# An eighth place in the ring of expert weights, in the memory of the residual

## What is computed

```
pg = softmax(h @ w_rg + b_rg)                 # 4 groups, the best one is taken
sel = the 8 expert logits of that group
pe_top, e_idx = top_k(softmax(sel), 2)        # 2 of 8 experts
weights = pg_top * pe_top / sum(pe_top)
for each token and each of its 2 experts:     # 32 experts in all
    a = xb @ w_gate[ex];  u = xb @ w_up[ex]   # 1024 x 512 each
    y = (silu(a) * u) @ w_down[ex]            # 512 x 1024
    out[token] += y * weight
x = x + out
```

## Time and profile before

| | before |
|---|---|
| median of 3 runs | 3719.6 us (3717.64 to 3726.79) |
| the profiled execution | 3721.73 us |
| its span in the trace | 3719.5 us |
| part on experts, first gate stage to last down stage | 3100.8 to 3692.3 us |
| PE busy, share of the span | 89% |
| DMA, mean of the core's 16 engines over six repetitions (3201.6 to 3647.4 us) | share 0.93, 388 GB/s |

### The profile page before, as it was taken

The page is one execution under the profiler, slowest core; times in us unless marked ns, Lnnn a source line. Parts: engine busy times, 40 slices in busy tenths (PEclk is TensorE's granted clock), DMA queues, the critical chain, the costliest instruction groups (busy, mean ns, idle before and its releaser), DMA issues.

```text
span 3719.5 us, 38781 instructions
## 1 busy us (share of the span) xinstructions
PE 3326.3 (89%) x16196; PEld 2288.9 (62%) x16196; DVE 1128.7 (30%) x1781; ACT 1053.8 (28%) x1795; POOL 709.1 (19%) x344
## 2 busy tenths in 40 slices
PE   7998899987858999989889999988899988989996
PEld 5676678865537777756568876465686664333332
DVE  5333320223395555353231112375230121000001
ACT  3532342325432222123342331133321122111110
POOL 3022244432210000013134440000242221000001
PEclk9999999997879988789999999998999999999998
DMA  3231153321100000122122323210122238989996
GB/s 117 80 124 46 46 185 109 125 85 51 57 12 1 1 2 1 51 94 77 36 86 94 91 91 96 78 35 1 38 90 71 74 149 324 401 355 392 386 387 279
DMA packets 217628, 448.04 MB, mean 120 GB/s; under 512 B 14176, under 2 KB 191360, under 8 KB 204528
## 3 DMA queue, kind: packets, MB, share of 16 engines
q1 hardware_dynamic: 197664, 389.04, 28.7%
q10 hardware_dynamic: 9744, 36.18, 2.4%
q0 software_dynamic: 10048, 20.35, 1.6%
HBM read 502.14 MB, written 31.46 MB: 143 GB/s over the span
## 4 chain that ended last, share of the span: by engine, by line
PE 77%; DVE 8%; DMA 8%; ACT 3%; issue 3%; POOL 1%; SPq 0%; ACTq 0%; POOLq 0%; DVEq 0%
PE product_banks L563 13%; PE product_banks L564 12%; PE product_banks L565 12%; PE product_banks L535 8%; PE product_banks L1923 5%; DMA A<-in_w_down 4%; PE product_banks L1960 4%; DMA A<-in_w_up 3%; PE product_banks L627 3%; PE product_banks L1125 1%; PE score_banks L1106 1%; PE product_banks L1342 1%; PE product_banks L2396 1%; PE product_banks L586 1%; PE product_banks L587 1%
## 5 line engine op out<-in xcount | busy, mean ns | idle before, releaser
L472 POOL TENSOR_TENSOR Wr_parts<-Wr,Wr_parts 128x1024 fp32r<-128x1024 f32 x186 | 447.1, 2405 | 1431.9 <-ACT Wr_parts L449 1431.9
L564 PE MATMUL product_banks<-A_parts,Wr_parts 128*128 128x512 f32 x1408 | 560.0, 398 | 0.0
L449 ACT ACTIVATE Wr_parts<-Wr 128x1024 fp32r<-128x1024 f32 x186 | 196.0, 1058 | 729.8 <-PE product_banks L565 634.8
L1923 PE MATMUL product_banks<-A,Wr 128*64 128x512 f32 x1504 | 344.3, 600 | 12.9 <-DMA A<-in_w_up 11.8
L563 PE MATMUL product_banks<-H_parts,Wr_parts 128*128 128x512 f32 x728 | 298.6, 410 | 24.4 <-POOL Wr_parts L472 20.8
L564 PEld LDWEIGHTS product_banks<-A_parts,Wr_parts 128*128 128x128 f32 x1408 | 270.0, 192 | 61.7 <-issue 2.2
L563 PE MATMUL product_banks<-A_parts,Wr_parts 128*128 128x512 f32 x680 | 269.5, 396 | 31.8 <-DVE A_parts L485 15.6
L565 PE MATMUL product_banks<-H_parts,Wr_parts 128*128 128x512 f32 x728 | 292.3, 402 | 0.0
L472 POOL TENSOR_TENSOR shared_con_parts<-Wr,shared_con_parts 128x1024 fp32r<-128x1024 f32 x80 | 193.0, 2413 | 449.8 <-ACT shared_con_parts L449 449.8
L565 PE MATMUL product_banks<-A_parts,Wr_parts 128*128 128x512 f32 x680 | 267.2, 393 | 0.0
L1923 PEld LDWEIGHTS product_banks<-A,Wr 128*64 128x64 f32 x1504 | 117.2, 138 | 216.9 <-issue 213.5
(11 more groups left out here) (444 smaller groups left out, 5246.1 us busy)
## 6 DMA issues: line engine op xcount, KB each, us to landing
A<-in_w_gate SPq DMA_DIRECT2D x32, 2048.0 KB, 14.0
A<-in_w_up SPq DMA_DIRECT2D x32, 2048.0 KB, 17.8
A<-in_w_down SPq DMA_DIRECT2D x32, 2048.0 KB, 13.6
Wr<-in_m_w_up SPq DMA_DIRECT2D x32, 1024.0 KB, 5.4
Wr<-in_m_w_down SPq DMA_DIRECT2D x32, 1024.0 KB, 4.7
Wr<-in_w_in SPq DMA_DIRECT2D x32, 1024.0 KB, 5.4
Wr<-in_c_w_kv SPq DMA_DIRECT2D x16, 1024.0 KB, 5.0
expert_rows<-LB ACTq DMA_DIRECT2D x12, 1024.0 KB, 4.4
```

Source lines behind the costliest of these rows:

```text
L449: nc.scalar.activation(weight_parts(s)[0], loaded_part(s), ACT.Copy).then_inc(*mark("weights_high", s))
L472: nc.gpsimd.tensor_tensor(lo, loaded_part(s), hi, ALU.subtract).then_inc(*mark("weights_split", s))
L564: pe.matmul(bank[:, :], hi[:, k, :], x_lo, start=False, stop=False)
L1923: mm = pe.matmul(BK[r, 0 if kind == "gate" else 1, :], XT[b % 2][:, k * P + CAP * h:k * P + CAP * h + CAP], unit_rows((kind, b, h))[:, k, ...
```

## The change

The ring has eight places. The first seven units go into the same places of `A` as before, the eighth into `X`, and so on round the ring; the load of unit g now waits for the stage that used unit g-8. The eighth unit, the first to use `X`, waits for the last turn of the residual.

```
-RINGW = 7
+RINGW = 8
...
         def unit_slot(key):
-            n = 8 * ((LOAD_AT[key] + 2) % RINGW)
-            return A[:, n:n + 8, :]
+            place = (2, 3, 4, 5, 6, 0, 1, 7)[LOAD_AT[key] % RINGW]
+            return X[:, :, :] if place == 7 else A[:, 8 * place:8 * place + 8, :]
...
                      ("low_part_ready", ("merged", 7)), ("products_done", ("wout2", 7)),
-                     ("products_done", ("wout2", 7))]
+                     ("products_done", ("wout2", 7)), ("turned", ("xr", TT - 1, 1))]
```

## The result

The changed kernel takes 3692.94 us (median of 4 runs, 3689.66 to 3695.72), the kernel before 3723.19 us over 4 runs. The ratio is 0.9918, 95% interval 0.9897 to 0.9939: 0.8% or 30 us faster. 3686 was forecast, with a range of 3667 to 3705.

The account below looks back on a forecast made before the run. Neither TensorE (66.9 us) nor DMA (66.3 us) alone but their waiting for each other was taken to bound each 74.3 us repetition. 35 us over six plus 1 at the start, leaned to 34, from 3719.6 gave 3686 us, range 3667 to 3705.

Parts of the forecast that it names:

- The circle: In the six repetitions, a down unit's late load idles the DMA and delays the next down stage; 7.4 us lost each.
- rivals C and E: C: DMA's sustained rate of 388 GB/s binds, gain 8 us at most, chance 0.06. E: TensorE alone binds, 3668 us, chance 0.07.
- The size: Six repetitions of nine expert stages: period 68.5 us instead of 74.3, 35 us gained in all.
- The DMA's idle: Experts, before the gate units issued at a down stage's end: 2.1 us idle instead of 7.4 per repetition.
- Rival B: Experts: the stall moves, DMA goes dry twice a repetition, period 71.5 us, gain 17 us, 3703 us; chance 0.13.
- The circle of 10 units: From one down stage's end to the down start three blocks on: 10 units, rows and restart, 60.0 us.
- The slow stage: Down stage partly at low clock, 8.4 us: disappears if the wait before it stays under 1.4 us.
- Rival D: Experts: several short waits, each followed by a low-clock stage; period 79.8 us, 33 us slower, 3753 us; chance 0.04.
- The start: Experts before 3201.6 us, one wait of 5.21 us and a slow stage: gain 0 to 7.9 us, taken as 1.
- Cost of nothing: Reading X as a place, POOL's wait for the turns and later row loads: each 0 us; 13 us bound for X.
- The signs: Profile after: period near 68.5 us, shorter down waits, adjacent SP issues, DMA 410 to 420 GB/s; wrong if full stretches fall below 427.

## Why the prediction was right

**The place of the loss.** The circle (a down unit that waits for the down stage, which waits for its own late unit) was read from the earlier trace rows. With the second half's wait put back the gain is gone, ratio 1.000; with X as a place but seven of them it is gone too. Shown. One slip in the working: the DMA's own loss was 74.3 - 66.3 = 8.0 us a repetition; the 7.4 that the prediction gives for it is TensorE's.

**The bounds of a repetition.** 66.3 us were worked out for the DMA alone and 66.9 for TensorE alone. Measured with the other out of the way: 66.6 and 67.0. So the 7.4 us that belonged to neither were real, and rivals C and E are judged by the same two numbers: there was something to gain, and a place does not get all of it.

**The size.** 68.5 us a repetition was forecast and 69.2 measured: 30.5 us over six instead of 35; at the end I had taken 2 off. The DMA's idle was forecast at 2.1 us. It measured 69.2 - 66.6 = 2.6 us a repetition by the periods and 2.3 by the rates. The size is near, but the place is wrong in the main. I had it in front of the gate that waits for the end of down; there it is 4.0 us in six repetitions. 9.4 us lie where I had none, in front of the down units that come behind an extra block's gate and up: empty units hold four of the eight places there, and the queue is nearly empty when those two units go out. The prediction let the last unit of down 5 land 3.9 us after that moment (3258.7 against 3254.8); it landed 1.9 us after it (3255.3 against 3253.4), and the two units behind it came too late to keep the rate up. Rival B said that the DMA runs dry in two places, which is so, but its second place was in front of gate 9, and there the rate hardly falls (399 GB/s from 3286 to 3292).

The circle of 10 units lacks the same term. It gave 60.0 to 60.8 us from the end of a down stage to the start of the one three blocks on. Where TensorE did not wait that took 60.1 us, its own eight stages (3264.3 to 3324.4); where it waited it took 61.6 to 63.2 (3401.7 to 3463.2, 3331.4 to 3394.6). So four waits of 1.4 to 3.1 us remained, where the forecast had 0 to 0.8, and a slow stage in two repetitions, where it had one in all or in none. Per repetition that is 67.0 + 1.5 of waits + 0.6 of slow stages = 69.1. That 69.2 is also the value worked out for a slow stage in every repetition is luck: the terms differ and their sum agrees.

**The slow stage.** I had tied its end to a wait under 1.4 us. It ended in four of six repetitions: in two there was no wait, and in one the wait was 1.44 us. The fourth is against the rule, and against my leaning on every wait above 2 us for a slow stage: waits of 2.17 and 2.34 us were followed by stages of 8.78 us, one of 3.08 us by a stage of 7.09, with the granted clock at 1.00 in it (3394.6 to 3401.7):

```profile
3394.57 7.09 PE L1960 MATMUL product_banks<-A,Wr 128*64 128x512 f32 x32 [3.08 <-DMA A<-in_w_down]
```

Rival D, many short waits with a slow stage behind each, did not come: there are fewer waits, not more. The experiment with six places shows that its mechanism exists (waits before gate with slow stages behind), though there it is the ring that causes them.

**The start.** The stage behind the long wait of the earlier trace rows now waits 2.95 us instead of 5.21 and takes 8.78 us instead of 9.78, but the down stage of block 2 waits 2 us where it hardly did before. From the first gate stage to 3201.6, 1.6 us were gained (3102.4 to 3201.6 against 3100.8 to 3201.6), where 1 us was forecast. In this profile that gain does not reach the time, since the first gate stage itself starts 1.6 us later than in the profile before.

**Cost of nothing.** X as a place, POOL's wait for the turns, the row transfers: all 0. Loads of rows land in 10.5 us at the median, 10.8 before.

**The signs.** Period, SP's issues, share, rate and the length of stages came as listed. One did not: the wait of down was to be under 1 us in at least half of the repetitions, and it was in two of six. And by the letter one sign of being wrong did come: the rate in full stretches was not to fall below 427 GB/s, and of six stretches of 32 us in the changed kernel four show 418 to 426, the others 427 and 429. It cost little: by the measured floor, at 424 GB/s, the transfers of a repetition take 66.6 us instead of 66.3.

The time of 3693 against 3686 has two parts: 4 us of gain that did not come (34 forecast, 30 measured), and the kernel before itself, whose median over the later runs is 3 to 4 us above the 3719.6 that I started from.

## What to carry to other kernels

When two engines are each busy for over nine tenths and the period is still longer than either one's own work, look for a circle: a wait in the queue that leads back to the stage which waits for that queue. Count the transfers that stand between the two waits. That count times one transfer, with the row traffic, the restart of the queue, the slowed stage and the 0.8 us by which the sum fell short with seven places added, gives the period here to within 2%, with six, seven and eight places, and tells roughly what one more place is worth. It does not tell where the waits stand: with six places new ones came before gate, and with eight the queue ran low in front of the down units. And measure both floors, one with half of the products, one without the ring's limit. They show that the next step is the start of a stage on half of its data, which with eight places brought the period to within 0.3 us of TensorE's own, at no memory.

In a ring that is ordered by use, units that may turn out empty cost depth as full ones do.

## What the runs showed of the hardware

One core's DMA moved 424 GB/s for 333 us, with unit loads, row loads and stores mixed. A 2 MB transfer in an empty queue landed 8.4 us after its issue, 3.5 us more than its bytes need at 427 GB/s, though a second unit issued 0.4 us behind it shared the engines. With only the last bytes of one unit left in the queue the rate fell before the next unit moved: SP issued at 3461.8, the unit before landed at 3463.0, and from 3460 to 3464 the DMA did 204 GB/s. The length of a wait of TensorE alone did not tell whether the next stage ran partly at the low clock: behind 2.17 us the granted clock was 0.81 over the stage, behind 3.08 us it was 1.00. Why is open.
